# Two-layer transformer kernel: the fp32r split of a weight slab placed one step earlier in the second block's layer

## The reference, cut to what matters

```python
def hybrid_layer(x, c_silu, cos, sin, norm_g, w_ada, b_ada, w_in, sinks, w_br_a, w_br_b, w_br_c, w_out):
    ...
    u = rms_norm_2(x, norm_g) * (1 + scale[:, None]) + shift[:, None]
    z = u @ w_in
    (aq, ak, av, ag, iq, ik, iw, bq, bk, bv, bg, cq, ck, cv, cg, ma, mb, mc) = jnp.split(z, SPLIT_OFFSETS, axis=-1)
    ya = dsa_attention(...)            # per query the top 128 keys by an index score, then softmax
    yb = swa_sinks_attention(...)      # window of 128 keys, with sinks
    yc = stick_breaking_attention(...) # exp(log_beta + reversed cumulative sum), 8 heads
    merged = (jax.nn.sigmoid(ma) * (ya @ w_br_a) + jax.nn.sigmoid(mb) * (yb @ w_br_b) + jax.nn.sigmoid(mc) * (yc @ w_br_c))
    return x + gate[:, None] * (merged @ w_out)
```

## Time and profile before

| | us |
|---|---|
| Median of three runs (3966.38 to 3968.31) | 3968.3 |
| The profiled execution, whole | 3965.53 |
| Its span in the profile | 3963.7 |
| PE busy in the span | 3568.3 (90%) |
| DVE busy | 1742.8 (44%) |
| ACT busy | 1106.0 (28%) |
| First step of the stage in its first and second pass | 2402.9 and 3187.7 |

### The profile page before, as it was taken

The page is one execution under the profiler, slowest core; times in us unless marked ns, Lnnn a source line. Parts: engine busy times, 40 slices in busy tenths (PEclk is TensorE's granted clock), DMA queues, the critical chain, the costliest instruction groups (busy, mean ns, idle before and its releaser), DMA issues. The chain is left out here.

```text
span 3963.7 us, 44746 instructions
## 1 busy us (share of the span) xinstructions
PE 3568.3 (90%) x17344; PEld 2400.9 (61%) x17344; DVE 1742.8 (44%) x3006; ACT 1106.0 (28%) x1719; POOL 105.4 (3%) x66
## 2 busy tenths in 40 slices
PE   7999987999978999987999967989899889898998
PEld 6766673444457766674444445656666766566666
DVE  5466633122166456533122163357643333575433
ACT  3333321011043333321011044323332143333321
POOL 1000000000031000000000030000000000000000
PEclk8999998999997999998999988989999989899999
DMA  3321128999942321138999942111112221111122
GB/s 118 109 85 55 65 103 350 423 424 424 410 160 99 119 77 54 67 126 348 423 423 424 375 170 96 53 43 54 59 66 78 97 82 52 43 64 59 70 75 96
DMA packets 123354, 645.80 MB, mean 163 GB/s; under 512 B 19956, under 2 KB 30196, under 8 KB 56088
## 3 DMA queue, kind: packets, MB, share of 16 engines
q1 hardware_dynamic: 123160, 643.18, 41.3%
HBM read 632.60 MB, written 14.72 MB: 163 GB/s over the span
## 5 line engine op out<-in xcount | busy, mean ns | idle before, releaser
L1556 PE MATMUL ps<-normed_T_hi,ring_split 128*128 128x512 f32 (+1 forms) x1952 | 637.8, 409 | 42.3 <-PEq L258 15.9
L1556 PEld LDWEIGHTS ps<-normed_T_hi,ring_split 128*128 128x128 f32 (+1 forms) x1952 | 369.3, 192 | 155.7 <-issue 46.1
L1556 PE MATMUL ps<-normed_T_lo,ring_split 128*128 128x512 f32 (+1 forms) x976 | 387.8, 397 | 0.0
L2200 PE MATMUL ps<-normed_T_hi,ring_split 128*128 128x512 f32 x1024 | 336.2, 410 | 9.0 <-DVE branches L2462 7.6
L1832 DVE TENSOR_TENSOR ring_split<-weight_ring,ring_split 128x2048 fp32r<-128x2048 f32 x76 | 174.0, 2289 | 301.3 <-ACT ring_split L1717 301.3
L2200 PEld LDWEIGHTS ps<-normed_T_hi,ring_split 128*128 128x128 f32 x1024 | 193.0, 192 | 82.6 <-issue 32.7
L1556 PEld LDWEIGHTS ps<-normed_T_lo,ring_split 128*128 128x128 f32 (+1 forms) x976 | 187.3, 192 | 42.5
L2200 PE MATMUL ps<-normed_T_lo,ring_split 128*128 128x512 f32 x512 | 202.9, 396 | 0.0
L1612 PE MATMUL ps<-branches 128*128 128x512 f32 x384 | 173.0, 593 | 2.2 <-DVE work L1906 2.2
L1200 PE MATMUL ps<-weight_ring,projected 128*64 128x512 f32 x768 | 167.9, 593 | 0.0
L1717 ACT ACTIVATE ring_split<-weight_ring 128x2048 fp32r<-128x2048 f32 x76 | 144.7, 1907 | 37.1 <-DMA weight_ring<-in_w_slabs 29.0
(11 more groups left out here) (422 smaller groups left out, 6426.3 us busy)
## 6 DMA issues: line engine op xcount, KB each, us to landing
weight_ring<-in_w_slabs SPq DMA_DIRECT2D x78, 1024.0 KB, 4.8
weight_ring<-in_w_exp_gate SPq DMA_DIRECT2D x48, 1024.0 KB, 16.5
weight_ring<-in_w_exp_down SPq DMA_DIRECT2D x48, 1024.0 KB, 12.7
weight_ring<-in_w_exp_up SPq DMA_DIRECT2D x48, 1024.0 KB, 20.2
weight_ring<-in_w_branch_gate SPq DMA_DIRECT2D x32, 1024.0 KB, 4.9
spare_weights<-in_w_exp_up SPq DMA_DIRECT2D x32, 1024.0 KB, 21.4
spare_weights<-in_w_exp_gate SPq DMA_DIRECT2D x32, 1024.0 KB, 20.7
spare_weights<-in_w_exp_down SPq DMA_DIRECT2D x32, 1024.0 KB, 16.1
```

The lines of the kernel that those rows point to most:

```text
L1556: ins = e.matmul(dst, lhs(k, m), rhs(k, m), start=k == 0 and m == 0, stop=k == KD - 1 and m == 2)
L2200: ins = e.matmul(dst, lhs(k, m), rhs(k, m), start=k == 0 and m == 0, stop=k == KD - 1 and m == 2)
```

## The change

The key under which a slab stands in `starts` becomes the step before the first step of the slab. The test in the two `dense` functions is as it was, so the split of slab q+1 is now done when ACT and DVE come to the step before the first step of slab q, ahead of the eviction of the step before that one.

```diff
@@ -1474,7 +1474,7 @@
                 if "slab" in st:
                     first_of.setdefault(st["slab"], i)
                     last_of[st["slab"]] = i
-            starts = {i: q for q, i in first_of.items()}
+            starts = {max(i - 1, 0): q for q, i in first_of.items()}
```

## The result

The changed kernel takes 4039.3 us (median of 4 runs, 4038.8 to 4040.6) against 3967.8 us before (4 runs). The ratio is 1.0183, with a 95% interval from 1.0169 to 1.0197: 71.5 us slower. The profiled execution took 4039.42 us, its span is 4037.6 us, 73.9 us longer than the span before.

The account below looks back on a forecast made before the run. PE was taken to set the time, busy 719.8 of 785 us. Per layer, 31.5 us of gaps and 9.7 of clock made 41.2, twice 82, giving 4051 us for the median; range 4015 to 4075.

Parts of the forecast that it names:

- first front: Splits 3 and 4: PE's wait at step 6 goes, a gain of 6.5 us and about 1.7 for clock per layer.
- second front: Split 5, now ahead of step 8's eviction: step 10 waits, a loss of 5.4 us and 2.2 for clock.
- fifth front: Split 10, now ahead of step 24's eviction: step 26 waits 6.6 us; net loss 3.9, no clock price.
- splits 18 and 19: Moved to steps 60 and 62, delaying DVE's picks and PE's transpose: a loss of 5.4 us and 2.2 for clock.
- split 20: Moved from step 73 to 72, delaying an eviction and normalizing by 5.8 us: net loss 4.6, and 1.5 for clock.
- split 21: Moved from step 77 to 76: takes 1.0 us off a later wait.
- splits 23 and 24: Moved to steps 82 and 83, ACT waiting for slab 24's landing: largest loss, 8.4 us and 2.2 for clock.
- clock term: PE's matmuls run slower after idle gaps: 9.7 us per layer on top of the gaps' 31.5.
- The rival without the clock term: The gaps come but the clock does not fall: +63 us, 4031 us; chance 0.17.
- Absorption: Rival: later waits absorb the delays from step 26 to step 73: +30 us, 3998 us; chance 0.10.
- Transfers as the wait: Rival: landings take 2 us longer and hold ACT at gate and out steps: +22 on top, 4073 us; chance 0.08.
- The faster rival: Elsewhere DVE finishes evictions before the moved split, so only gains count: -21 us, 3947 us; chance 0.04.

Follow-up runs that it names:

- The first two experiments: Against the kernel before: splits 3 and 4 alone at the earlier step, 3950.0 us; then split 5 alone at the earlier step, 3980.2 us.
- The best placement found: Against the kernel before: only ACT's high halves moved earlier, except those of splits 9, 13 and 24; DVE's low halves at their old steps; 3938.7 us.
- the kernel that is 24 us slower: Against the kernel before: all of ACT's high halves at the earlier step, DVE's low halves at their old step; 3962.7 us.

## Why the prediction was right, and where it was off

The forecast of 4051 us and its direction held; the measured 4039.3 lies 12 us below it, and 71.5 us stand where 83 were forecast. The mechanism was the one described. The table compares the starts of PE's steps in the first pass of the two traces (by the timeline, steps 0 to 123, less the 0.4 us by which the stage starts later). Each row is what the lag grew by across a place, the clock included. In the second pass, 37.9 us in all, each place lies within 1.3 us of its row:

| place | forecast | measured |
|---|---|---|
| first front | -8.2 | -8.5 |
| second front | 7.6 | 7.0 |
| third front | 7.6 | 6.9 |
| fourth front | 0 | 0.6 |
| fifth front | 3.9 | 4.3 |
| sixth front | 2.8 | 2.7 |
| seventh front | 1.9 | 1.4 |
| step 47 | 3.4 | 3.6 |
| splits 18 and 19 | 7.6 | 6.6 |
| split 20 | 6.1 | 4.7 |
| split 21 | -1.0 | -2.0 |
| splits 23 and 24 | 10.6 | 9.8 |
| the rest | -1.1 | -1.2 |
| sum | 41.2 | 35.9 |

**The places at the fronts**, copied from positions in the code and from the times at which DVE's rows end, were right to a microsecond each. The first two experiments priced two of them alone: 16.7 and 13.5 us for two passes, where the table has 17.0 and 14.0.

**The terms that were mis-sized** are those of the attend items: splits 18 and 19, 20, 21, 23 and 24. Their sum was put at 23.3 us per pass, and it measured 19.1; that is 4.2 of the 5.3 us. The delays themselves came out as forecast: the transposes behind split 19 moved by 4.9 us (forecast 5.4), those behind split 20 by 6.0 (5.8), the second ones behind split 24 by 8.2 (8.4). Too large was the clock price added on top of them, 2.2, 1.5 and 2.2 us. Behind these transposes the lag grew by only 1.7, 0.1 and 1.7 us more, which is 2.4 us less. At split 20 one sees why: the gap grew from 1.90 to 5.99 us, by 4.1, while the transposes moved by 6.0. PE's small matmuls ahead of them had already run slower (the last two took 1.74 us where they took 1.12), so that price lay inside the delay and was counted a second time. And I gave split 21 half of what it brings: the whole wait of 1.92 us for the normalizing of job 10 went.

**The clock.** The sum had 9.7 us per pass for it and 31.5 for the gaps. PE's busy time, for the same instructions, rose by 10.8 us in the first pass and by 21.7 us in all (3568.3 to 3590.0 us); idle PE made up the other 24.8 us of the first pass. So the clock term was right as a total, and the gaps were put too high: the delays that the sum lists as gaps were in part PE working at the lower clock. That the total was right is partly luck, since single steps do not keep to 2.2 us either: behind a gap of 5.8 us step 10 and step 14 cost 1.6 to 2.1 us more in the two passes of the changed kernel, and step 26 behind 6.46 us 2.8 and 1.9. The rival without the clock term, 4031 us, came nearer to the 4039.3 us by its time than the forecast did, 8 us off against 12. It is not the time that speaks against it but the trace: the granted clock of the first pass fell from 0.96 to 0.93, and 21.7 of the 73.9 us are busy PE. The rival hit its number because the forecast for the gaps, which it shares, was too high. The Trainium skill (TensorE: Matmul & The Clock Gate, What's actually happening) says that for modelling the ramp penalty is under 1% of a typical kernel span. This kernel differs: in the trace of before PE was busy for 249 us at the half clock, and with half of that taken as lost, an estimate, it is 125 us or 3% of the span. The added 21.7 us are 0.5% of the span, but 29% of the difference between the two kernels.

**The other rivals.** Absorption fell with the kernel whose middle was put back: 49.0 us came off, no less than the traces hold there. Transfers as the wait fell with the kernel of early high halves: the same waits for landings, and 76.7 us less; nor did the transfers get slower, a slab lands in 4.8 us as before. A landing matters in one place, split 24, where it holds ACT and through it DVE, as the sum had it: 18.1 us. The faster rival was wrong about the second front, but right that there is something to win at the first.

## What to carry to other kernels

When a preparation step is moved to an earlier place in an engine's program, list what now stands behind it in that queue and whether its input is there when the engine comes to it; its own deadline may not press at all, as here, where PE waited for a low half of this stage in none of the eleven traces. A step of two halves on two engines need not move as one: the half that waits for the other should stand where the other has long finished. Such places can be priced one by one from a trace and then chosen one by one: the same 37 moves gave +1.8% together, and a selection of their first halves -0.7%.

## What was not expected

The best placement found left DVE idle for 136.6 us ahead of its low halves, against 125.3 us in the kernel that is 24 us slower. And the kernel with the eviction first has 214.4 us of it, less than the 301.3 of the kernel before, and is 34 us slower. The idle time of DVE follows the harm between the first two kernels, but it does not rank the kernels: only the idle time which PE then waits behind counts. The exchange of two lines, eviction before split, which removed all new waits at four fronts as foreseen, was worth only half of what the whole change cost, since the split then waits for PE's step ahead of it.
